# Squares by head on ScalarE, one denominator step per tile, and moved work in the first tiles of a transformer layer

## The reference

```python
shift1, scale1, gate1, shift2, scale2, gate2 = split(silu(c) @ w_ada + b_ada, 6)
h = rmsnorm(x, norm1_gain) * (1 + scale1) + shift1
q, k, v, p = split(h @ w_in)               # 512, 128, 128, 512 columns
q = rmsnorm(q per head of 64, q_gain); k = rmsnorm(k per head, k_gain)   # 8 and 2 heads
attn = softmax([q.k / 8 + bias, sink]) @ v # window of two 64-token chunks
pool = (mean over 2/4/8/16 tokens - self) @ w_pool * pool_scale
x = x + gate1 * (concat(rmsnorm(attn), rmsnorm(pool)) @ w_out)
h2 = rmsnorm(x, norm2_gain) * (1 + scale2) + shift2
out = x + gate2 * ((silu(h2 @ w_gate) * (h2 @ w_up)) @ w_down)
```

## Time and profile before

| | us | share of the span |
|---|---|---|
| median of three executions | 962.2 | |
| the profiled execution | 962.17 | |
| its span, first to last instruction | 960.4 | 100% |
| TensorE busy | 925.4 | 96% |
| VectorE busy | 789.3 | 82% |
| ScalarE busy | 521.0 | 54% |
| GpSimd busy | 283.8 | 30% |

### The profile page before, as it was taken

One profiled execution on the slowest core, in us unless ns is written; L12 is line 12 of the kernel. 1 busy time (PEld: TensorE's weight loads), 2 busy tenths in 40 slices (PEclk: granted clock), 3 DMA queues, 4 the chain that ended last, 5 costly groups with the idle time before them and its releaser, 6 DMA issues.

```text
span 960.4 us, 14014 instructions
## 1 busy us (share of the span) xinstructions
PE 925.4 (96%) x4327; PEld 760.3 (79%) x4327; DVE 789.3 (82%) x1239; ACT 521.0 (54%) x1006; POOL 283.8 (30%) x243
## 2 busy tenths in 40 slices
PE   7988999989999998999999999999999999999998
PEld 6647788778887777888888888888888888888886
DVE  4949999999689968888787977879698787977797
ACT  4544655576345645555464654646465464655543
POOL 0025455432100100703306061240704215070334
PEclk9999999999999999999999999999999999999999
DMA  9965754338345495557456556644656556455624
GB/s 359 390 214 158 281 176 154 110 122 274 132 129 179 142 328 209 197 202 259 152 195 227 210 178 218 220 173 175 227 198 231 196 186 229 175 183 210 219 88 176
DMA packets 96135, 193.97 MB, mean 202 GB/s; under 512 B 6512, under 2 KB 57440, under 8 KB 96096
## 3 DMA queue, kind: packets, MB, share of 16 engines
q1 hardware_dynamic: 90816, 182.05, 54.2%
q10 hardware_dynamic: 5280, 11.45, 3.3%
HBM read 176.30 MB, written 17.17 MB: 201 GB/s over the span
## 4 chain that ended last, share of the span: by engine, by line
PE 71%; DVE 17%; issue 4%; DMA 3%; ACT 3%; POOL 1%; SPq 1%; ACTq 0%; DVEq 0%; POOLq 0%
PE ps L2173 23%; PE ps L2174 23%; PE ps L2175 23%; DVE stage L1404 2%; DMA raw_u<-in_w_up 1%; DVE wo_raw L1500 1%; DVE ada_in_raw L1404 1%; DMA x_st<-in_x 1%; DVE nmax L1645 1%; DMA wi_raw<-in_w_in 1%; DVE acc L1417 1%; DVE s_sb L1644 1%; DVE wi_lo L1588 1%; DVE wo_lo L1505 1%; PE ps L2426 1%
## 5 line engine op out<-in xcount | busy, mean ns | idle before, releaser
L1348 POOL TENSOR_TENSOR x<-x,p1s 128x512 f32<-128x512 f32 x80 | 117.0, 1483 | 422.4 <-ACT p1s L1045 421.6
L2173 PE MATMUL ps<-bs,ring 128*128 128x512 f32 x344 | 134.2, 390 | 3.3 <-ACT ps L973 2.6
L2175 PE MATMUL ps<-bs,ring 128*128 128x512 f32 x344 | 133.9, 389 | 0.0
L2174 PE MATMUL ps<-bs,ring 128*128 128x512 f32 x344 | 133.8, 389 | 0.0
L1787 DVE TENSOR_TENSOR ring<-s,ring 128x512 fp32r<-128x512 f32 x88 | 68.7, 799 | 50.0 <-ACT ring L966 50.0
L2173 PE MATMUL ps<-h_hi,ring 128*128 128x512 f32 x272 | 106.1, 390 | 0.6 <-DVE h_lo L1780 0.6
L2174 PE MATMUL ps<-h_lo,ring 128*128 128x512 f32 x272 | 105.8, 389 | 0.0
L2175 PE MATMUL ps<-h_hi,ring 128*128 128x512 f32 x272 | 105.8, 389 | 0.0
L966 ACT ACTIVATE ring<-s 128x512 fp32r<-128x512 f32 x88 | 53.8, 623 | 66.5 <-PE ps L2175 66.5
L2173 PEld LDWEIGHTS ps<-bs,ring 128*128 128x128 f32 x344 | 64.6, 188 | 18.1 <-issue 3.4
L2173 PE MATMUL ps<-wi_hi,ht_hi 128*128 128x512 f32 (+1 forms) x192 | 71.0, 370 | 7.9 <-DVE ht_lo L1547 2.3
(11 more groups left out here) (302 smaller groups left out, 2344.2 us busy)
## 6 DMA issues: line engine op xcount, KB each, us to landing
bs<-bs_scratch SPq DMA_DIRECT2D x166, 512.0 KB, 6.2
raw_g<-in_w_gate SPq DMA_DIRECT2D x11, 1024.0 KB, 5.3
raw_u<-in_w_up SPq DMA_DIRECT2D x11, 1024.0 KB, 7.7
raw_d<-in_w_down SPq DMA_DIRECT2D x20, 512.0 KB, 4.2
ada_in_raw<-in_w_adat SPq DMA_DIRECT2D x16, 512.0 KB, 11.1
stage<-in_w_adat SPq DMA_DIRECT2D x16, 512.0 KB, 5.7
wi_raw<-in_w_in SPq DMA_DIRECT2D x8, 640.0 KB, 12.3
stage<-in_w_ada SPq DMA_DIRECT2D x8, 512.0 KB, 4.6
```

What stands on the lines that cost most here:

```text
L1348: pool.tensor_tensor(x1_half(t, 1), x1_half(t, 1), p1s[j][:, :], ALU.add).then_inc(pool_evac, 1)
L2173: pe.matmul(dst, s_hi, m_hi, start=start, stop=False, skip_group_check=onto)
L2174: pe.matmul(dst, s_hi, m_lo, start=False, stop=False, skip_group_check=onto)
L2175: return pe.matmul(dst, s_lo, m_hi, start=False, stop=stop, skip_group_check=onto)
```

## The change

Five things. The squares of q and k are taken on ScalarE in ten instructions, one a head, each of which also gives its sum; VectorE's reduction and the semaphore between fall away, and the next tile's squares wait for the inverse roots. The addition and reciprocal of both score halves are done once, after both halves' exponentials. The normalised k is written twice by one instruction with broadcast operands. In the first tiles work is moved: `shift_high` and `h_high(2)` ahead of `square_x(1)`; `scale_x(3)`, `h_high(3)` and `h_low(3)` from turn 0 to the end of turn 1; folds 0 to 2 ahead of `evac_q(0)`, with FOLDS and TAKEN changed; the gate bias loads behind the first four pieces, which are issued one by one as the shift columns free the ring's room; the last projection block of tile 1 behind the shift parts. And eight filler products (`keep_busy_gap`) stand behind block row 0.

```diff
-        FOLDS = (3, 4, 4, 5, 4, 4, 0, 0)
+        FOLDS = (3, 3, 4, 5, 4, 5, 0, 0)
-        TAKEN = {3: GATE1, 4: SCALE2, 6: SHIFT2}
+        TAKEN = {3: GATE1, 5: SCALE2, 6: SHIFT2}
...
             load_xt(2)
-            sp.dma_start(g1bc[:, :], b_ada[0, GATE1 * D:(GATE1 + 1) * D].partition_broadcast(P)).then_inc(gate_in, 16)
-            sp.dma_start(g2bc[:, :], b_ada[0, GATE2 * D:(GATE2 + 1) * D].partition_broadcast(P)).then_inc(gate_in, 16)
             sp.wait_ge(hlo_done, KT + 1)
             load_xt(3)
-            sp.wait_ge(shift_sum, KT)
             for n, (mm, k) in enumerate(pieces):
-                if n >= RING:
+                if n < RING:
+                    sp.wait_ge(shift_sum, KT - RING + n + 1)
+                else:
                     sp.wait_ge(ada_used, n - RING + 1)
+                if n == RING:
+                    for bc, gate in ((g1bc, GATE1), (g2bc, GATE2)):
+                        sp.dma_start(bc[:, :], b_ada[0, gate * D:(gate + 1) * D].partition_broadcast(P)).then_inc(gate_in, 16)
...
                 act.wait_ge(kv_evac, t + 1)
                 if t >= 1:
-                    act.wait_ge(ssqk_done, t)
-                act.activation(sq_qk[:, :, :].rearrange("p h d -> p (h d)"), qkv[:, 0:QW + NKV * HD], ACT.Square
-                               ).then_inc(sqqk_done, 1)
+                    act.wait_ge(rsqk_done, t)
+                for h in range(NQ + NKV):
+                    last = act.activation(sq_qk[:, h, :], qkv[:, h * HD:(h + 1) * HD], ACT.Square, accum_out=ss_qk[:, h:h + 1])
+                last.then_inc(ssqk_done, 1)
...
             square_x(0)
-            shift_high(KT - 4)
-            shift_high(KT - 3)
-            square_x(1)
-            for j in range(KT - 2, KT):
+            for j in range(KT - 4, KT):
                 shift_high(j)
             h_high(2)
+            square_x(1)
             constants()
...
                     square_qk(it)
-                if it == 0:
-                    h_high(3)
...
                     square_x(it + 2)
+                if it == 1:
+                    h_high(3)
...
+            def denominators(a):
+
+                dve.wait_ge(exp_done, 2 * a + 2)
+                link(dve.tensor_tensor(den[:, :, :], rowsum[:, :, :], sinkex[:, :, :], ALU.add))
+                link(dve.reciprocal(rden[:, :, :], den[:, :, :]))
+
             def probs(a, ch):
 
-                dve.wait_ge(exp_done, 2 * a + ch + 1)
-                link(dve.tensor_tensor(den[:, ch, :], rowsum[:, ch, :], sinkex[:, ch, :], ALU.add))
-                link(dve.reciprocal(rden[:, ch, :], den[:, ch, :]))
...
                     h_low(2)
-                    scale_x(3)
+                    fold(0)
+                    fold(1)
+                    fold(2)
                     evac_q(0)
...
-                    dve.wait_ge(sqqk_done, it + 1)
-                    dve.tensor_reduce(ss_qk[:, :], sq_qk[:, :, :], AX.X, ALU.add).then_inc(ssqk_done, 1)
+                    dve.wait_ge(kv_evac, it + 1)
...
-                if it == 0:
-                    fold(0)
...
+                    denominators(a)
                     probs(a, 0)
                     probs(a, 1)
...
-                    for d in range(2):
-                        last = dve.tensor_tensor(kn[:, :, d, :], kv,
-                                                 rs_qk[:, NQ:].unsqueeze(2).broadcast_to([P, NKV, HD]), ALU.mult)
-                    last.then_inc(qkn_done, 1)
+                    dve.tensor_tensor(kn[:, :, :, :], kv.unsqueeze(2).broadcast_to([P, NKV, 2, HD]),
+                                      rs_qk[:, NQ:].unsqueeze(2).unsqueeze(3).broadcast_to([P, NKV, 2, HD]), ALU.mult
+                                      ).then_inc(qkn_done, 1)
...
                     bias_tiles()
-                    h_low(3)
-                    fold(1)
...
+                if it == 1:
+                    scale_x(3)
                 if it < NT:
-                    for n in range(sum(FOLDS[:it]) if it else 2, sum(FOLDS[:it + 1])):
+                    for n in range(sum(FOLDS[:it]) if it else 3, sum(FOLDS[:it + 1])):
                         fold(n)
+                    if it == 1:
+                        h_low(3)
...
+            def keep_busy_gap(n):
+                for _ in range(n):
+                    pe.matmul(bank(6)[:, 0:P], ones[:, :], ones[:, :], start=True, stop=True)
...
                     project_block(1, j)
+                    if j == 0:
+                        keep_busy_gap(8)
...
                 project_block(0, KT - 1)
-                project_block(1, KT - 1, (1,))
...
                     shift_part(part, range(KT - 3, KT))
-                project_block(1, KT - 1, (0, 2))
+                project_block(1, KT - 1, (1, 0, 2))
```

More of the change, by code:

```diff
@@ L349, in build_program @@
         q_evac, kv_evac, p_evac = sem("q_evac"), sem("kv_evac"), sem("p_evac")
-        sqqk_done = sem("sqqk_done")
         ssqk_done = sem("ssqk_done")
```

## The result

| | time, us | ratio to before | 95% interval |
|---|---|---|---|
| before | 962.15 | | |
| changed | 971.44 | 1.0098 | 1.0085 to 1.0111 |

The changed kernel is slower by 9.3 us, 1.0%. The forecast of 963.1 us, with its range to 968.0, missed it. The profiled execution of the changed kernel took 969.85 us, so its trace shows 7.7 of the 9.3 us.

What follows compares the result with a forecast made beforehand. VectorE's stream was taken to bound the kernel up to 185 us. From 4.85 us early entering turn 3, the terms summed to +0.5 at h_low(7), +1.2 at turn 7's scores and +0.9 at 217 us: 963.1 us, range 957.5 to 968.

Steps and rivals of the forecast that it cites:

- The bound (VectorE's stream up to 185 us): Whole kernel: VectorE's stream sets the time up to 185 us; behind 217 us TensorE runs on alone.
- Ten squares at 0.245 us each: ScalarE, each tile: ten squares by head take 2.45 us, 1.8 more than before; bounds 1.5 and 3.9 us.
- The first rival: Cheap squares on ScalarE: reads of the sums overlap, ten heads cost 1.5 us, total 958.3 us; chance 0.14.
- The second rival: Dear squares on ScalarE: 0.39 us a head, 3.9 us for ten, total 970.5 us; chance 0.10.
- VectorE's stall of 1.8 us in it 3 to 6: Turns 3 to 6: longer squares delay ScalarE's h_high, so VectorE stands still before h_low, 1.8 us each turn.
- from −4.85 to +0.5: VectorE's lead of 4.85 us on entering turn 3 becomes 0.5 us of lateness at h_low(7).
- TensorE's wait at tile 7: Before tile 7's q columns TensorE waits about 4.3 us for h_low(7), formerly 1.79; half clock behind costs 1.7 us.
- The single denominator waits 0.3 us: VectorE, per turn: the one denominator now waits for both exponential groups, 0.3 us of waiting.
- The filler gains 1.4 us: First projection, behind block row 0: eight filler products hold the clock at 2.4 GHz, gaining 1.4 us; bounds 0 and 1.6.
- So square and issue end at 51.9 us and the constants start 1.8 us earlier: ScalarE before the shift rows: moving shift_high and h_high(2) ahead of square_x(1) starts the constants' DMA issues 1.8 us earlier.
- The projection block's 0.5 us: Before the shift rows: the projection block no longer stands between TensorE and them, worth 0.5 us.
- Only 3.4 us earlier, behind a TensorE gap of some 4 us: Turn 2: ScalarE's h_high(3) waits for scale_x(3), so transposes of q come at 84.0 us, not 87.37.

Runs made afterwards that it cites:

- e5: The kernel before with only one addition and reciprocal for both denominators and k normalised in one instruction: 957.44 us, ratio 0.9958.
- e15: The kernel before with only the eight filler products behind block row 0 added: 960.46 us, ratio 0.9990.
- e7: The kernel of e1 with 20 filler products between TensorE's last projection block and the shift rows: 961.51 us, ratio 0.9991.
- e13: The changed kernel with SyncE holding gate biases and later pieces until the first shift row is on its way: 965.37 us, ratio 1.0043.
- e10: The kernel of e1 with SyncE held until the first shift row and tile 3 prepared in turn 0 again (late moves undone): 953.16 us, ratio 0.9904.
- e1: The changed kernel with the squares undone (one square of 640 columns on ScalarE, reduction on VectorE): 961.13 us, ratio 0.9998.
- e14: The changed kernel with ten filler products on TensorE before the q columns of tiles 5 and 7: 969.68 us, ratio 1.0097.

## Why the prediction was wrong, step by step

- The bound (VectorE's stream up to 185 us): right. All that the runs won or lost came through it.
- Ten squares at 0.245 us each: right, 2.40 us. The first rival rested on the Trainium skill, page "ScalarE: Activation LUTs", section "What ACT_TABLE_LOAD costs"; the trace agrees with its duration for 64 columns (0.24 us) and with the overlap of 93 ns, which is there at each pair: the read of the sum starts 0.09 us before its square ends, and the next square 0.09 us before the read ends. What the rival lacked is the read itself, 0.18 us less its overlap, 0.09 more a head. The second rival's 970.5 us is near the measured 971.4 us by luck: its mechanism, 0.39 us a head, did not happen.
- VectorE's stall of 1.8 us in it 3 to 6: right (6.9 us in four). From entering it 3 to `h_low(7)` I worked out +5.35 us (from −4.85 to +0.5), and the trace has +5.2 (from +0.2 at 114.43 to 189.04 against 183.69). TensorE's wait at tile 7 was 2.7, not 4.3, and half clock stood behind it. That the sum came out may in part be luck, since one of its terms is mis-sized: I counted the denominators and k at 0.16 us a turn net (0.46 less 0.3 of waiting), and alone they save 0.9 (e5).
- The single denominator waits 0.3 us: 0.2 in it 3 to 6, but 1.4 in it 2, where the exponentials come behind `h_high(3)`'s wait and the squares.
- The filler gains 1.4 us: the clock is right, the columns were 1.1 us earlier, and alone it gains nothing (e15).
- **"So square and issue end at 51.9 us and the constants start 1.8 us earlier"**, with their length taken as before: this is the step that failed. The start was right (51.9 less the filler's 1.4 is 50.5, measured 50.69) and the length was not, 6.4 us for 4.5. I had costed each queue for itself, ScalarE's issues by their own rows. That the moved loads of SyncE could lengthen them I put at nothing, and the collision of the bias with the fold pieces at below 1 us. The first shift row is 2.5 us later than forecast (57.11 for 54.6) and the first scores 4.3 (74.60 for 70.3). With SyncE held they are 0.3 and 0.4 late. So most of the lost lead hangs on the issues; why 2.3 us at the shift row become 3.9 at the first scores is argued only (the TensorE wait of 4.2 us and the low clock behind it), since e7 did not test it. e13 prices the step at 5.3 us by the ratios and 3.9 at the marks: without it the kernel takes 965.4, inside the range, 2.3 above the forecast.
- The projection block's 0.5 us: not seen. With SyncE held the constants start 3.3 us earlier than before and the shift row comes 3.4 us earlier.
- "Only 3.4 us earlier, behind a TensorE gap of some 4 us" in it 2: the gap was 4.25 us, as said. With the longer issue the transposes came 0.9 us later than before (88.30 for 87.37), with SyncE held 2.9 earlier. Of the 2.3 us left, 1.2 lie here and in it 2: e13 enters it 3 with a lead of 3.7, not 4.85.
- The chances gave slower 0.34, and no mechanism in that third was the true one. A rival "the moved loads of SyncE make ScalarE's issues longer" was missing.

## What to carry to other kernels

Before an instruction on an in-order engine gets longer, look at what stands behind it that doesn't need it, and at the idle time ahead of it: here a copy of 1.06 us fitted into 4.3 us of idle time ahead of the squares, and its place was worth 8.5 us. DMA issues cost time on the engine that makes them, and here that time depended on what another queue had issued in the few us before; when loads are moved earlier, compare the issue times of all queues in that stretch. And time parts one by one: this change held a gain of 4 us (denominators and k), one of 3 us by the traces and 5 by the ratios (the early part, once SyncE is held: e10 against e5), and three losses that hid them (the issue of the constants, tile 3 moved, the squares' place).

## What the runs showed of the hardware

- The same seven DMA issues on ScalarE took 4.4 to 5.0 us in the fourteen kernels where SyncE issued nothing then, and 6.0 to 9.2 us in the six where it issued five transfers of 512 KB in the same stretch; single ones went from 0.53 to 1.66 us and from 0.63 to 3.50 (e13, e1). In the eight held kernels a single issue of SyncE took 3.9 to 5.9 us while ScalarE issued nothing.
- A square of 64 columns: 0.24 us, the read of its sum 0.18 to 0.19, and 0.24 from square to square, since each instruction starts 0.09 us before the one ahead of it ends. A square of 640 columns held ScalarE for 0.65, and the reduction took VectorE 0.81.
- A wait of TensorE of 1.77 us left the clock at 2.4 GHz, one of 2.71 us was followed by seven products at 1.2 GHz. A wait of 1.88 us behind small filler products (e14) was followed by five products at 2.4 GHz and then eight at 1.2. Giving the clock back in one of the two stretches did not move the time.
